# A decoder layer on one core: three experts chosen from early counts, loads by first use, and a new order of places

## What is computed

```python
h2 = rms_norm(x1) * (1 + sc_f) + sh_f
g_logits = h2 @ w_rg + b_rg                      # 4 groups
g_star = argmax(g_logits)
in_group = logits of the 8 experts of g_star
top_v, top_i = top_k(in_group, 2)
gate_w = softmax(top_v) * softmax(g_logits)[g_star]
# each token goes to 2 of 32 experts
y_e = (silu(x @ w_gate[e]) * (x @ w_up[e])) @ w_down[e]   # 1024 -> 512 -> 1024
f = sum over its two experts of gate_w * y_e
out = x1 + gt_f * rms_norm(f)
```

## Time and profile before

| | |
|---|---|
| median of 3 runs | 1735.85 us (1732.85 to 1741.08) |
| profiled execution | 1732.28 us |
| its span | 1730.4 us |
| TensorE busy | 1620.1 us, 94% |
| VectorE, ScalarE, GpSimd busy | 44%, 36%, 8% |
| DMA | 404.62 MB, mean 234 GB/s |

### The profile page before, as it was taken

The page is one execution under the profiler, slowest core; times in us unless marked ns, Lnnn a source line. Parts: engine busy times, 40 slices in busy tenths (PEclk is TensorE's granted clock), DMA queues, the critical chain, the costliest instruction groups (busy, mean ns, idle before and its releaser), DMA issues. The chain is left out here.

```text
span 1730.4 us, 27681 instructions
## 1 busy us (share of the span) xinstructions
PE 1620.1 (94%) x11350; PEld 1155.0 (67%) x11350; DVE 755.3 (44%) x1392; ACT 630.0 (36%) x1195; POOL 130.0 (8%) x219
## 2 busy tenths in 40 slices
PE   6999888999999999999999999969999999999984
PEld 3889767888888889999999989743333333333331
DVE  4524346888888764454455464751000000000006
ACT  4535435666655553343534353311111111111112
POOL 0000011111111000000000030000000000000001
PEclk9999989999999999999999999979999999999997
DMA  9463461111111285373447564379999999999977
GB/s 371 164 209 131 168 212 35 53 53 45 48 53 53 77 289 189 128 267 129 164 139 253 180 209 141 115 313 428 425 425 396 426 427 427 423 425 387 372 300 302
DMA packets 97156, 404.62 MB, mean 234 GB/s; under 512 B 12503, under 2 KB 40439, under 8 KB 84088
## 3 DMA queue, kind: packets, MB, share of 16 engines
q1 hardware_dynamic: 84768, 380.23, 57.6%
q0 software_dynamic: 7248, 17.71, 2.6%
q10 hardware_dynamic: 5016, 4.93, 1.0%
HBM read 365.29 MB, written 44.84 MB: 237 GB/s over the span
## 5 line engine op out<-in xcount | busy, mean ns | idle before, releaser
L1157 ACT ACTIVATE wup<-wraw 128x1024 fp32r<-128x1024 f32 x120 | 126.7, 1059 | 264.2 <-PE ps L1957 226.2
L1617 DVE TENSOR_TENSOR wlow<-wraw,wup 128x1024 fp32r<-128x1024 f32 x120 | 146.7, 1224 | 155.6 <-ACT wup L1157 155.3
L1957 PE MATMUL ps<-wg,xT 128*32 128x512 f32 (+2 forms) x1200 | 160.0, 595 | 5.2 <-DMA wg<-w_gate 4.0
L1957 PE MATMUL ps<-wd,aT 128*32 128x512 f32 (+2 forms) x1200 | 155.5, 593 | 9.3 <-DMA wd<-w_down 7.9
L1957 PE MATMUL ps<-wu,xT 128*32 128x512 f32 (+2 forms) x1200 | 155.6, 594 | 1.1 <-DMA wu<-w_up 1.0
L1957 PE MATMUL ps<-h_up,wup 128*128 128x384 f32 (+1 forms) x384 | 124.7, 325 | 3.5 <-DVE wlow L1617 3.5
L1957 PEld LDWEIGHTS ps<-wd,aT 128*32 128x32 f32 (+2 forms) x1200 | 48.5, 114 | 112.8 <-issue 111.1
L1957 PE MATMUL ps<-h_up,wlow 128*128 128x384 f32 (+1 forms) x384 | 123.6, 322 | 0.0
L1957 PE MATMUL ps<-h_low,wup 128*128 128x384 f32 (+1 forms) x384 | 123.6, 322 | 0.0
L1957 PEld LDWEIGHTS ps<-wg,xT 128*32 128x32 f32 (+2 forms) x1200 | 45.9, 114 | 100.1 <-issue 97.7
L1957 PEld LDWEIGHTS ps<-wu,xT 128*32 128x32 f32 (+2 forms) x1200 | 47.1, 114 | 93.9 <-issue 91.8
(11 more groups left out here) (393 smaller groups left out, 3340.9 us busy)
## 6 DMA issues: line engine op xcount, KB each, us to landing
wg<-w_gate SPq DMA_DIRECT2D x32, 2048.0 KB, 16.5
wu<-w_up SPq DMA_DIRECT2D x32, 2048.0 KB, 14.8
wd<-w_down SPq DMA_DIRECT2D x32, 2048.0 KB, 16.2
wraw<-w_ga SPq DMA_DIRECT2D x24, 512.0 KB, 3.6
wraw<-w_gr SPq DMA_DIRECT2D x24, 512.0 KB, 3.8
wraw<-w_at SPq DMA_DIRECT2D x24, 512.0 KB, 3.6
wraw<-w_lr SPq DMA_DIRECT2D x24, 512.0 KB, 3.5
wraw<-w_out SPq DMA_DIRECT2D x24, 512.0 KB, 3.6
```

The lines of the kernel that those rows point to most:

```text
L1157: act.activation(wup[n % UP][:, :, :], wraw[n % RAW][:, :, :], ACT.Copy).then_inc(w_rounded, 1)
L1617: V.tensor_tensor(wlow[n % RAW][:, :, :], wraw[n % RAW][:, :, :], wup[n % UP][:, :, :].bitcast(F32), ALU.subtract).then_inc(w_split, 1)
L1957: return pe.matmul(out, lhsT, rhs, start=start, stop=stop, skip_group_check=True)
```

## The change

`CAPS` gets another order of the same numbers: 84 quarters in 21 rounds and 4 in the tail as before. Places 0, 1 and 2 have two quarters each and take the three lowest ranks. Which experts they are is settled early: TensorE counts the tokens of tiles 0 to 5 (`EARLY` = 6), VectorE ranks these counts (`early_places`, `early_choice`) and writes `eid0`; in the final ranking the keys of these three are lowered by a multiple of `LOW`, so that they get the last ranks whatever their counts. SP issues the loads of place 0 and the gate of place 2 ahead of the x1 and h2 stores, those of place 1 behind them, the up and the down of place 2 behind the first gather and the tables. The other loads are sorted by first use. The G2 rows are loaded behind the tail's loads. The rows of every block, that of the tail too, are turned a round ahead, and the tail loop turns the next rows at its end. The slot tables are computed behind the preparation of the weights, and the product for the weights comes before the first turning. Fillers are added around the turnings and logits of the last tiles and ahead of the closing sums. Tiles 0, 1, 5 and 8 are summed on VectorE, the others on TensorE.

```diff
--- before.py
+++ after.py
...
-CAPS = (3, 3, 3, 3, 3, 2, 2, 2, 6, 2, 2, 4, 2, 3, 2, 3, 3, 2, 3, 2, 4, 2, 2, 2, 6, 2, 2, 3, 2, 2, 2, 4)
+CAPS = (2, 2, 2, 2, 3, 4, 2, 4, 2, 3, 3, 2, 2, 6, 2, 2, 2, 3, 3, 3, 3, 3, 2, 3, 6, 2, 2, 3, 2, 2, 2, 4)
...
-BY_PE = [1, 2, 4, 5, 7]
-BY_DVE = [0, 3, 6, 8]
+BY_PE = [2, 3, 4, 6, 7]
+BY_DVE = [0, 1, 5, 8]
...
-SIZED = sorted(range(NE), key=lambda n: -CAPS[n])
+SIZED = sorted(range(NE), key=lambda n: (-CAPS[n], n < SETS))
...
+EARLY = 3 * (GRP - 1)
+LOW = 65536.0
+assert [PLACE_RANK[n] for n in range(SETS)] == list(range(NE - SETS, NE))
...
-    when = {"gate": lambda n: (LAST[n] - 1, 1), "up": lambda n: (LAST[n], 0), "down": lambda n: (LAST[n], 2)}
-    first = [(n, kind) for n in range(SETS) for kind in ("gate", "up", "down")]
-    later = [(when[kind](n - SETS), n, kind) for n in range(SETS, TAIL) for kind in ("gate", "up", "down")]
-    return first + [(n, kind) for _, n, kind in sorted(later, key=lambda t: t[:2])]
+    first_use = {"gate": lambda n: (FIRST[n] - 1, 1), "up": lambda n: (FIRST[n], 0), "down": lambda n: (FIRST[n], 2)}
+    return [(n, kind) for _, n, kind in sorted((first_use[kind](n), n, kind) for n in range(SETS, TAIL) for kind in ("gate", "up", "down"))]
...
+            def first_weights(n, kinds):
+                r = PLACE_RANK[n]
+                e = sp.value_load(eid0[r:r + 1, 0:1], min_val=0, max_val=NE - 1)
+                for kind in kinds:
+                    w, ld, done = buffers[kind]
+                    sp.dma_start(w[n][:, :, :], weights(kind, e)).then_inc(ld[n], 16)
...
             sp.wait_ge(step_done, STEP["lr", GRP - 1, KC - 1] + 1)
+            sp.wait_ge(early_ready, 4)
+            first_weights(0, ("gate", "up", "down"))
+            first_weights(2, ("gate",))
             for t, j, n in tiles(GRP - 1):
                 x1_store(t, j, n)
             for t, j, n in tiles(GRP - 1):
                 h2_store(t, j, n)
+            first_weights(1, ("gate", "up", "down"))
...
-            spread_rows(1, 2, G2p, 0)
...
+            sp.wait_ge(rows_asked, 1)
+            first_weights(2, ("up",))
+            sp.wait_ge(tables, 4)
+            first_weights(2, ("down",))
             for n, kind in expert_loads():
                 w, ld, done = buffers[kind]
                 r = PLACE_RANK[n]
                 e = sp.value_load(eid[r:r + 1, 0:1], min_val=0, max_val=NE - 1)
-                if n >= SETS:
-                    sp.wait_ge(done, LAST[n - SETS] + 1)
-                if (n, kind) == (SETS - 1, "down"):
-                    sp.wait_ge(tables, 4)
+                sp.wait_ge(done, LAST[n - SETS] + 1)
                 sp.dma_start(w[n % SETS][:, :, :], weights(kind, e)).then_inc(ld[n % SETS], 16)
...
+            spread_rows(1, 2, G2p, 0)
+            for b in range(NB):
+                sp.dma_start(G2s[NT * b:NT * (b + 1), :].rearrange("p (h n) -> p h n", h=2),
+                             mod_dram[1, 2:4, 1 + b:2 + b, :].rearrange("h r n -> r h n").broadcast_to([NT, 2, 512])).then_inc(ld_spread, 16)
...
+            sp.wait_ge(x_low_half, trips + ROUNDS + 1)
+            sp.wait_ge(x_high_half, trips + ROUNDS + 1)
...
             gather(0)
+            pool.sem_inc(rows_asked, 1)
             gather(1)
...
-                if n + 1 < ROUNDS:
-                    keep_x(n + 1)
+                keep_x(n + 1)
...
+            def early_places():
+                dve.wait_ge(order_pe, 1)
+                k(V.tensor_copy(cnt0[:, :], ps[:, 3, 0:NE]))
+                k(V.scalar_tensor_tensor(key0[:, :], cnt0[:, :], float(NE), iot[:, 0:NE], ALU.mult, ALU.subtract))
+                k(V.tensor_tensor(kdiag0[:, :], key0[:, :], ident[:, 0:NE], ALU.mult))
+                k(V.tensor_reduce(kcol0[:, :], kdiag0[:, :], AX_X, ALU.add))
+                V.tensor_scalar(lower0[:, :], key0[:, :], kcol0[:, 0:1], None, ALU.is_lt).then_inc(early_ready, 1)
+
+            def early_choice():
+                dve.wait_ge(order_pe, 2)
+                V.tensor_scalar(ohrank0[:, :], ps[:, 3, 0:NE], row0[:, 0:1], None, ALU.is_equal).then_inc(early_ready, 1)
+                V.tensor_scalar(lowered[:, :], ps[:, 3, 0:NE], float(NE - SETS - 1), 0.0, ALU.subtract, ALU.max).then_inc(early_ready, 1)
+                dve.wait_ge(early_ready, 3)
+                k(V.tensor_tensor(eprod0[:, :], ohrank0[:, :], iot[:, 0:NE], ALU.mult))
+                k(V.tensor_reduce(kcol0[:, :], eprod0[:, :], AX_X, ALU.add))
+                V.tensor_copy(eid0[:, :], kcol0[:, :]).then_inc(early_ready, 1)
+                k(V.scalar_tensor_tensor(lowered[:, :], lowered[:, :], LOW, iot[:, 0:NE], ALU.mult, ALU.add))
...
                 if q == 4:
                     choose(0, 3 * last)
                 if q == 4:
+                    early_places()
...
+            early_choice()
             last_half(0)
             last_x1(0)
             last_half(1)
...
-            k(V.scalar_tensor_tensor(key[:, :], cntf[:, :], float(NE), iot[:, 0:NE], ALU.mult, ALU.subtract))
+            k(V.scalar_tensor_tensor(key[:, :], cntf[:, :], float(NE), lowered[:, :], ALU.mult, ALU.subtract))
...
-            dve.wait_ge(rt_pe, 2)
-            k(V.tensor_scalar(slf[:, :], ps[:, 6, MAXB:2 * MAXB], float(4 * PLANE - 1), None, ALU.add))
-            k(V.scalar_tensor_tensor(slf[:, :], ps[:, 6, 0:MAXB], float(P), slf[:, :], ALU.mult, ALU.add))
-            k(V.tensor_tensor(slot_to[:, :], slf[:, :], most[:, :], ALU.min))
-            V.tensor_scalar(slot_from[:, 0:MAXB], slot_to[:, :], PLANE - 1, None, ALU.bitwise_and).then_inc(tables, 1)
             dve.wait_ge(rt_exp, 2)
             k(V.tensor_reduce(gsm[:, :], gex[:, :, :], AX_X, ALU.add))
...
+            dve.wait_ge(rt_pe, 2)
+            k(V.tensor_scalar(slf[:, :], ps[:, 6, MAXB:2 * MAXB], float(4 * PLANE - 1), None, ALU.add))
...
+            def first_order():
+                pe.wait_ge(early_ready, 1)
+                mm(ps[:, 3, 0:NE], ubf[0:NE, 1, :], lower0[0:NE, :], True, True).then_inc(order_pe, 1)
+
+            for q in range(KC - 1):
                 mix(last, q)
             pe.wait_ge(rt_ready, 1)
+            for b in range(EARLY):
+                ins = mm(ps[:, 3, 0:NE], ubf[:, 1, :], ohs[:, b, :], b == 0, b == EARLY - 1)
+            ins.then_inc(order_pe, 1)
+            mix(last, KC - 1, first_order)
             rank(0, 3 * last)
...
                 turn(last, j, 0, (4, 0, 4)[j])
-                turn(last, j, 1, (5, 3, 5)[j])
+                turn(last, j, 1, (5, 2, 5)[j])
+                keep_warm(5)
                 if j:
                     pe.wait_ge(mix_kept, 6 * last + 4 + j)
                     pe.wait_ge(mix_sq, 6 * last + 4 + j)
-                logits(last, j, ((6, 1, 2)[j], 0), (h2T, h2Tb, h2T)[j])
+                if j == 2:
+                    pe.wait_ge(lg_kept, 3 * last + 1)
+                logits(last, j, ((6, 1, 6)[j], 64 * (j // 2)), (h2T, h2Tb, h2T)[j])
+                if j < 2:
+                    keep_warm(6)
...
-            keep_warm(30)
+            keep_warm(24)
...
-            turn_rows(0)
             pe.wait_ge(rt_ready, 6)
             for q in range(TK):
                 n = rows(q // 2)
                 ins = mm(ps[:, 7, 0:3 * MAXB], ohslot[0:n, q, :], rhs3[0:n, q, :, :].rearrange("p a b -> p (a b)"), q == 0, q == TK - 1)
             ins.then_inc(rt_pe, 1)
+            turn_rows(0)
...
+                turn_x(LATE).then_inc(xg_used, 1)
+            keep_warm(90)
```

More of the change, by code:

```diff
@@ L1285, in _ @@
                 for part in range(2):
-                    keep_turned(last, j, part, ((0, 3), (4, 5))[j - 1][part], (h2Tb, h2T)[j - 1], 1)
+                    keep_turned(last, j, part, ((0, 2), (4, 5))[j - 1][part], (h2Tb, h2T)[j - 1], 1)
             act.wait_ge(ld_route, 112)
@@ L1812, in _ @@
             for j in (1, 2):
-                keep_logits(last, j, ((1, 2)[j - 1], 0))
+                keep_logits(last, j, ((1, 6)[j - 1], 64 * (j - 1)))
             dve.wait_ge(lg_kept, TILES)
@@ L2229, in product, with mix @@
                 ins.then_inc(step_done, 1)
-            def mix(g, q):
+            def mix(g, q, behind_first=None):
                 n, hf, kp = STEP["out", g, q], q // 4, q % 4
@@ L2255, in mix @@
                         ins.then_inc(step_done, 1)
+                    if j == 0 and behind_first is not None:
+                        behind_first()
             def turn(g, j, part, at):
```

59 lines of the change are left out of this document (34 added, 25 removed).

## The result

| | before | after |
|---|---|---|
| median of 14 runs, us | 1736.03 (1730.45 to 1741.67) | 1726.81 (1718.37 to 1733.49) |
| ratio | | 0.9946, interval 0.9933 to 0.9958 |
| profiled execution, us | 1732.28 | 1727.51 |
| its span, us | 1730.4 | 1725.7 |

The change saves 9.2 us. The prediction said 1709, 27 less, with a range of 1698 to 1724: the sign was right, the size was not, and the time lies above the range.

What follows compares the result with a forecast made beforehand. Weight loads, slightly longer than TensorE's stream beside them, bound the rounds; -9.2 up to the second turning, +0.6 and -10.9 in rounds, -1.1 tail, -4.0 closing sums make -24.6: 1707.7 profiled, 1709 as median, range 1698 to 1724.

Steps and rivals of the forecast that it cites:

- Early choice: Counting and ranking around the last mix steps: mostly covered by VectorE's waits, +0.2 us (0 to 1.3).
- rival C: Early choice wrong: an expert above 64 rows adds a 23.4 us tail pass; 1732 or 1756; chance 2% each.
- Logits: Logits of the last three tiles: fillers in the gaps keep TensorE's clock up, -2.2 us.
- Slots: Slot tables behind the weights' preparation: nine VectorE operations go ahead of the wait for the slots, +0.4 us.
- First gather: First gather of rows: 6.4 us instead of 10.90 with a nearly empty queue, -4.5 (0 to -7.6).
- Round 0: First to second turning: 8.1 us instead of 11.2, product moved and clock up, -3.1 (0 to -3.1).
- rival B: The beginning gains little: clock falls (+4.2), round 0 slow (+1.5), gather no faster (+4.5); 1719 us; chance 14%.
- Rounds: Rounds 1 to 20: 2 us of waits for weights instead of 12.9, -10.9; more two-group rounds, +0.6.
- Rival A: Loads stay the bound in the rounds: 10 to 18 us of waiting left; 1721 us; chance 17%.
- Tail: Tail: last block's turning and copies move into round 20, TensorE's 1.07 us standstill goes, -1.1 us.
- Closing sums: Closing sums: tiles 0 and 1 on VectorE fill its 4.33 us idle hole, -4.0 us (-1 to -5).
- D: First gather keeps its 10.90 us, row after row and not the queue; 1713.5 us; chance 10%.

Runs made afterwards that it cites:

- r1: Changed kernel with the up weights of expert 2 issued when the first gather has landed, not when it is issued; 1724.09 us, ratio 0.9935.
- r2: Changed kernel with both gate and up weights of expert 2 issued only when the first gather has landed; 1726.30 us, ratio 0.9943.
- r10: Kernel before with only the new order of capacities and the loads sorted by first use; 1744.59 us, ratio 1.0053.
- r3: Changed kernel with 64 more fillers between the second slot product and the first turning; 1726.99 us, ratio 0.9943.
- r8: Changed kernel with expert 2's up held until the first gather lands, 26 fillers before the first turning, 150 before the closing sums; 1721.05 us, ratio 0.9898.
- r9: Changed kernel with the old split of the closing sums and 125 fillers ahead of them in place of 90; 1721.78 us, ratio 0.9907.
- r5: Changed kernel with the old split of the closing sums and its 90 fillers kept; 1725.68 us, ratio 0.9930.
- r7: Changed kernel with the first experts' loads issued only when the tables are ready, as before, new order kept; 1740.06 us, ratio 1.0018.
- r4: Changed kernel with 150 in place of 90 fillers ahead of the closing sums; 1727.27 us, ratio 0.9945.
- r6: Changed kernel with later loads sorted by the last use of their buffer, as before, new capacities kept; 1734.61 us, ratio 0.9986.

## Why the prediction was wrong in size

Step by step, in the prediction's order; measured numbers are from the anchor table and the fences above.

- **Early choice: right.** Forecast +0.2 with VectorE's waits as cover; ScalarE's idle time ahead of the anchor grew by 0.25. Both batches fit where they were placed, the loads start 2.1 us behind the anchor (forecast 1107, which is 3 behind 1104.00), and the tail loop ran once: rival C did not happen.
- **Logits: right.** -2.2 forecast. From the anchor to the addition of tile 8's logits it took 22.2 us before and takes 19.65: -2.5. The clock stayed at its upper level of 2.4 GHz in both batches (1.98 and 1.95 us).
- **Slots: right.** +0.4 forecast, +0.3 measured (from that addition to the slots).
- **First gather: the step that failed first.** Forecast 6.4, measured 10.84. The mechanism (the queue beside it) was right, as r1 and r2 show. The argument against it, from an even split between the queues, was not: packets of 4 KB take turns with packets of 16 KB. What failed is the sentence "only the end of expert 1 is left in the queue": the last of its loads landed at 1157.5, 4.9 us behind the gather's issue, and the next load, which waits only for the gather's issue and not for its landing, followed 0.6 us behind it. On before's scale (5.9 less) expert 1 landed at 1151.6 and not at the 1149 of my sum, and the gather was issued at 1146.7, 2 us earlier than before. I had the two ends nearly together and took that for a free queue. 4.4 us. The second half of the sentence, "the next load waits until the gather is issued", cost the most: holding that one load until the rows have landed gives 4.7 us (r1).
- **Round 0: failed.** Forecast 8.1, measured 12.2. The sum said "with the product moved and the clock up", and nothing held it up: TensorE has nothing to do for 7.42 us. Before, the small product stood behind the turning and took slow time on itself (1.97 in r10, and its gate then 7.09); with the product moved ahead, the gate runs slow instead (9.52), and the clock came back later. r3 gives 8.9 with fillers there. So of the 4.1 us 3.3 are the clock, and 0.8 are the gate's wait for the copy of the rows, which the sum left out. This was half of rival B: the gather was no faster and round 0 was slow, the logits went as forecast. But B had put only 1.5 us on round 0.
- **A gain at the beginning is not kept whole in round 1.** Nothing in the sum said so. The sum carried -9.2 at the second turning through to the end; r2 had -11.3 there and nothing left one round on. Even if the two steps above had come true, part of them could have been lost: up to the third turning r8 keeps 2.4 of 8.1 us and r1 5.1 of 6.3.
- **Rounds: right in mechanism, too optimistic by 3.1 us of waiting.** 12.9 of waits became 5.1 and not 2, most of it at two downs (1.78 and 2.21), and why at these two wasn't followed. Rival A (10 to 18 us left) did not happen. The stretch with the tail changed by -9.9 for a forecast of -11.4, so the products and turnings in it came out 1.6 us cheaper than my sum had them.
- **Tail: right.** The idle 1.07 us is gone.
- **Closing sums: failed.** -4.0 forecast, +0.6 measured. The 3.9 us were saved where the account put them, in VectorE's full stretch. The step that failed is the start of that stretch: I carried it forward with TensorE's first sum "some 4 us behind" the fillers and 1 us for a low clock. It was 6.01 us behind, because the first tile is now the third to land, and the cold first sum cost 3.1 us more than a warm one. F to R grew from 15.2 to 19.6, 4.4 us, and ate the gain; 3.5 of them are the later start, since the first sum was cold in the kernel before too. Part of the 4.6 us is this one trace: five others with the same closing code have a closing stretch 0.5 to 1.5 us shorter than before.

Together 4.4 + 4.1 at the beginning (0.4 of which logits and slots gave back), 1.5 in the rounds and 4.6 at the end make the 14 us that are missing. Added to 1709 they give 1723; another 2.3 are there because the profiled execution lay 3.6 below the median and I added only 1.3 of that, and 1.4 because the stretches of the two traces fell by 10.6 and the medians by 9.2. Most of the terms had been priced one by one, in rivals B and D and at the weak end of the closing sums. I had given their joint case too little. Two of them, round 0 and the first sum, share a cause: TensorE comes out of a wait for a DMA with a low clock. The rows of before showed it at the first turning, and the sum took the clock as up without naming anything that would hold it there.

What stays open: whether r9's time is more than luck, whether r8 or r1 is the better version, why the first packets of a gather start 2.5 us behind its issue in one case and 4.9 in another, and why the clock came back sooner where the small product stood behind the first turning.

## What to carry to other kernels

When a change lets a transfer start earlier, work out what is in the queue beside it at that very moment, and make the next bulk load wait for the landing and not for the issue. Where an engine's buffers are reused one round later, a gain at the start is capped by the first load that waits for a buffer: follow it to that load before it is summed. And where TensorE comes out of a wait with a low clock, the next work pays, whichever it is: taking a small product out of that place laid the slow time on the gate. Fill the wait up to the moment when the data come, and no further: ten us of fillers were not enough for a wait of sixteen, and r9's 125 held the sum back by some 0.8 us. A tile that the critical engine starts with should be one that lands early.

## What the runs showed of the hardware

- A gather of 128 rows (0.52 MB) took 10.84 us with two weight loads beside it, 6.13 with one, and 4.04 with no load. Beside the loads its 4 KB packets and their 16 KB packets came in equal numbers, 83 and 86 in 4 us, so the loads had 82% of the DMA engines' time.
- A 2 MB load with nothing in flight at its issue landed 7.3 to 8.9 us later, in most cases 8.1 to 8.3. Loads that follow each other with nothing between land 4.9 us apart (1151.07 and 1155.97 in r10). With one load and a gather in flight it took 9.5 (r1) and 11.5 (r8), with three loads 16.9 (r2), with four 22.0 (r10).
- After 7.42 us of standstill the turning took 1.97 for 1.16 us and the gate 9.52 for 7.09; after 6.01 the first sum took 6.66 for 3.57, and after 13.19 5.78. After 2.95 us the first sum lost nothing (r5), but after 2.82 and another 0.75 a gate took 8.76 for 7.09 (r1).
- A scaling on VectorE took 3.08 us beside GpSimd's addition and 1.29 without it.
- Single executions differ by up to 10 us before the change acts: the anchor lies between 1102.14 and 1112.12, and the spread is already there at VectorE's 200th operation, at 262.3 in r9 and 272.3 in r7. The granted clock of the first 40 us doesn't settle it: it was 0.96 in early ones (before, r1, r4, r6, r9) and 0.83 to 0.85 in late ones (after, r3, r7), but r8 had 1.00 and reached the anchor at 1109.11, and r10 had 0.79 and reached it at 1107.01.
